# Last feed-forward stage: high and low latent halves as one 512-column moving operand

## What is computed

```python
def ffn_half(h, mod, k0, norm_w, wg, wu, wd):
    u = modulate(rmsnorm(h, norm_w), mod[:, k0, None], mod[:, k0 + 1, None])
    y = (jax.nn.silu(u @ wg) * (u @ wu)) @ wd
    return h + 0.5 * mod[:, k0 + 2, None] * y
```

## Time and profile before

| | us |
|---|---|
| median of 3 runs (lowest, highest) | 1979.12 (1977.79, 1980.22) |
| the profiled execution, its own time | 1976.28 |
| its span | 1974.6 |
| TensorE busy | 1942.9 (98%) |
| TensorE weight loads busy | 1649.4 (84%) |
| VectorE busy | 1262.6 (64%) |
| ScalarE busy | 795.4 (40%) |
| chain that ended last: TensorE's share | 92% |

### The profile page before, as it was taken

The page is one execution under the profiler, slowest core; times in us unless marked ns, Lnnn a source line. Parts: engine busy times, 40 slices in busy tenths (PEclk is TensorE's granted clock), DMA queues, the critical chain, the costliest instruction groups (busy, mean ns, idle before and its releaser), DMA issues.

```text
span 1974.6 us, 29022 instructions
## 1 busy us (share of the span) xinstructions
PE 1942.9 (98%) x10024; PEld 1649.4 (84%) x10024; DVE 1262.6 (64%) x2048; ACT 795.4 (40%) x1083; POOL 72.7 (4%) x142
## 2 busy tenths in 40 slices
PE   7999999999999999999999999999999998999998
PEld 2888888888888888888888888888888897999998
DVE  3667576676665466667566675755757678575555
ACT  2422222345554323532222353223224576456444
POOL 0000000000000000000000000000100000000000
PEclk9999999999999999999999999999999999999999
DMA  7345445433223243345454534444544333545554
GB/s 311 107 150 190 139 162 177 158 105 111 71 69 112 87 139 121 111 139 202 138 160 168 161 96 151 169 160 141 205 140 129 99 105 105 178 149 182 183 184 154
DMA packets 78664, 287.39 MB, mean 146 GB/s; under 512 B 8768, under 2 KB 10048, under 8 KB 77824
## 3 DMA queue, kind: packets, MB, share of 16 engines
q1 hardware_dynamic: 58912, 212.89, 32.5%
q0 software_dynamic: 19392, 73.34, 11.4%
q10 hardware_dynamic: 288, 0.18, 0.0%
HBM read 285.34 MB, written 1.05 MB: 145 GB/s over the span
## 4 chain that ended last, share of the span: by engine, by line
PE 92%; DVE 3%; DMA 2%; issue 1%; ACT 1%; ACTq 0%; DVEq 0%; SPq 0%
PE bank L333 26%; PE bank L334 26%; PE bank L335 26%; DMA raw<-weights 2%; PE bank L689 1%; PE bank L496 1%; PE bank L556 1%; PE bank L550 1%; PE bank L551 1%; ACT w_hi L712 1%; DVE S L1186 1%; PE bank L633 1%; PE bank L361 1%; PE bank L417 1%; PE bank L411 0%
## 5 line engine op out<-in xcount | busy, mean ns | idle before, releaser
L333 PE MATMUL bank<-u_hi,w_hi 128*128 128x512 f32 (+1 forms) x1824 | 664.0, 364 | 0.4 <-DVE w_lo L980 0.4
L334 PE MATMUL bank<-u_lo,w_hi 128*128 128x512 f32 (+1 forms) x1824 | 654.7, 359 | 0.0
L335 PE MATMUL bank<-u_hi,w_lo 128*128 128x512 f32 (+1 forms) x1824 | 654.6, 359 | 0.0
L980 DVE TENSOR_TENSOR w_lo<-raw,w_hi 128x1024 fp32r<-128x1024 f32 x384 | 469.1, 1223 | 245.8 <-ACT w_hi L712 216.5
L712 ACT ACTIVATE w_hi<-raw 128x1024 fp32r<-128x1024 f32 x384 | 405.1, 1056 | 435.1 <-DMA raw<-weights 434.4
L333 PEld LDWEIGHTS bank<-u_hi,w_hi 128*128 128x128 f32 x1824 | 344.5, 189 | 51.5 <-DVE w_lo L980 1.0
L335 PEld LDWEIGHTS bank<-u_hi,w_lo 128*128 128x128 f32 x1824 | 344.3, 189 | 51.3
L334 PEld LDWEIGHTS bank<-u_lo,w_hi 128*128 128x128 f32 x1824 | 344.6, 189 | 50.3 <-issue 0.7
L333 PE MATMUL bank<-hid_hi,w_hi 128*128 128x512 f32 (+1 forms) x832 | 299.1, 360 | 0.7 <-DVE w_lo L980 0.5
L991 DVE SCALAR_TENSOR_TENSOR junk<-ada_raw,silu_c 128x1024 bf16<-128x1024 f32 x256 | 298.2, 1220 | 0.5 <-DVE junk L991 0.5
L335 PE MATMUL bank<-hid_hi,w_lo 128*128 128x512 f32 (+1 forms) x832 | 298.2, 358 | 0.0
(11 more groups left out here) (162 smaller groups left out, 1504.5 us busy)
## 6 DMA issues: line engine op xcount, KB each, us to landing
raw<-weights SPq DMA_DIRECT2D x384, 512.0 KB, 3.5
ada_raw<-adaw POOLq DMA_DIRECT2D x128, 512.0 KB, 4.3
start_w<-weights SPq DMA_DIRECT2D x8, 1024.0 KB, 12.5
box<-box POOLq DMA_DIRECT2D x4, 1024.0 KB, 8.0
h<-resid SPq DMA_DIRECT2D x1, 2048.0 KB, 19.5
silu_c<-c POOLq DMA_DIRECT2D x1, 1024.0 KB, 5.2
out<-sig_a SPq DMA_DIRECT2D x8, 128.0 KB, 2.0
poolw<-poolw POOLq DMA_DIRECT2D x2, 256.0 KB, 10.0
```

The source lines that it names most:

```text
L333: pe.matmul(ps, w_hi[:, slot, k, :], hi(k), start=first, stop=False)
L334: pe.matmul(ps, w_hi[:, slot, k, :], lo(k), start=False, stop=False)
L335: mm = pe.matmul(ps, w_lo[:, slot, k, :], hi(k), start=False, stop=last)
L980: dve.tensor_tensor(view(w_lo, (j % RING) * UNIT, [1, UNIT]), raw[:, j % RING, :], view(w_hi, (j % RING) * UNIT, [1, UNIT]).bitcast(F32), ...
```

## The change

`u_hi` and `u_lo` become two halves of one tensor, `u_both` (at the same addresses as before). In the last feed-forward block, gate and up units take two matmuls per k in place of three: the high weights against the high and the low activations as one moving operand of 2 x 256 columns, written to both halves of the 512-column bank, and the low weights against the high activations (256 columns), added to the first half of the bank. The first four k of `abreast` stay as they were. The two halves of a bank are added on the way out: ACT copies the second halves of the up bank and the gate bank into the unused second halves of `hid_t` and `silu_t`, DVE adds the first halves of the banks to them, then Silu and the product read these sums from SBUF. Two semaphores are new: `s_low` (ACT to DVE) and `s_sum` (DVE to ACT and to DVE itself). Down units and all blocks over 512 tokens are as before.

```diff
-        u_hi, u_hi_at = sb("u_hi", [P, ND, ALL], F32R)
-        u_lo, _ = sb("u_lo", [P, ND, ALL], F32R)
+        u_both, u_hi_at = sb("u_both", [P, 2, ND, ALL], F32R)
+        u_hi, u_lo = u_both[:, 0], u_both[:, 1]
...
+            def half_latent(ps, slot, k, start, stop):
+
+                pe.matmul(ps[:], w_hi[:, slot, k, :], view(u_both, k * ALL, [ND * ALL, 2], [1, TOK]), start=start,
+                          stop=False, skip_group_check=True)
+                return pe.matmul(ps[:, 0:TOK], w_lo[:, slot, k, :], u_hi[:, k, 0:TOK], start=False, stop=stop,
+                                 skip_group_check=True)
+
+            def unit_latent(ps, slot, unit_wait):
+
+                pe.wait_ge(s_lo, unit_wait - START)
+                for k in range(ND):
+                    mm = half_latent(ps, slot, k, k == 0, k == ND - 1)
+                mm.then_inc(s_used, 1)
...
                 for g in range(AHEAD):
                     for k in range(side_by_side, ND):
                         pe.wait_ge(s_ulo, at + k + 1)
+                        if nt == TOK:
+                            mm = half_latent(bank[g], g, k, False, k == ND - 1)
+                            continue
...
                     for j in (2 * b, 2 * b + 1):
+                        if ntok == TOK:
+                            unit_latent(bank[j], j, i * 4 + (base + j + 1))
+                            continue
                         half(bank[j][:, 0:ntok], j, 0, ND, hi, lo, i * 4 + (base + j + 1), done=True)
...
-                        half(bank[3][:, 0:ntok], 3, 0, ND, hi, lo, base + 4, done=True)
+                        if ntok == TOK:
+                            unit_latent(bank[3], 3, base + 4)
+                        else:
+                            half(bank[3][:, 0:ntok], 3, 0, ND, hi, lo, base + 4, done=True)
...
                             act.wait_ge(s_used, i * 4 + (base + 2 * b + 2))
-                            act.activation(silu_t[:, b, 0:nt], bank[2 * b][:, 0:nt], ACT.Silu).then_inc(s_silu, 1)
+                            if last_ffn:
+                                for n_bank, low in ((2 * b + 1, hid_t), (2 * b, silu_t)):
+                                    ins = act.activation(low[:, b, TOK:ALL], bank[n_bank][:, TOK:ALL], ACT.Copy)
+                                ins.then_inc(s_low, 1)
+                                act.wait_ge(s_sum, i * 2 + (hid - hid_count(layer, which) + b + 1))
+                                act.activation(silu_t[:, b, 0:nt], silu_t[:, b, TOK:ALL], ACT.Silu).then_inc(s_silu, 1)
+                            else:
+                                act.activation(silu_t[:, b, 0:nt], bank[2 * b][:, 0:nt], ACT.Silu).then_inc(s_silu, 1)
...
                             split_lo(base, i, 2 * b + AHEAD)
+                            if last_ffn:
+                                at_sum = i * 2 + (hid - hid_count(layer, which) + b + 1)
+                                dve.wait_ge(s_low, at_sum)
+                                for n_bank, low in ((2 * b + 1, hid_t), (2 * b, silu_t)):
+                                    ins = dve.tensor_tensor(low[:, b, TOK:ALL], low[:, b, TOK:ALL],
+                                                            bank[n_bank][:, 0:TOK], ALU.add)
+                                ins.then_inc(s_sum, 1)
+                                dve.wait_ge(s_sum, at_sum)
                             dve.wait_ge(s_silu, i * 2 + (hid + b + 1))
 
-                            dve.tensor_tensor(hid_t[:, b, 0:nt], silu_t[:, b, 0:nt], bank[2 * b + 1][:, 0:nt],
+                            up = hid_t[:, b, TOK:ALL] if last_ffn else bank[2 * b + 1][:, 0:nt]
+                            dve.tensor_tensor(hid_t[:, b, 0:nt], silu_t[:, b, 0:nt], up,
                                               ALU.mult).then_inc(s_up_free, 1)
```

More of the change, by code:

```diff
@@ L204, in program @@
         s_silu = sem("silu_ready")
+        s_low = sem("low_halves_out")
+        s_sum = sem("halves_added")
         s_hid_hi = sem("hid_hi_ready")
```

## The result

Over six runs each on the same chips the changed kernel took 1983.63 us (median, 1981.22 to 1987.11) against 1978.09 us (1975.88 to 1980.22): ratio 1.0032, 95% interval 1.0020 to 1.0043, so slower by 4.0 to 8.5 us, the lower end lying just on the 0.2% that the prediction took as the limit of what can be told. The forecast was 1984.2 us, with 0.60 on slower. The profiled execution took 1981.22 us in place of 1976.28.

What follows compares the result with a forecast made beforehand. TensorE, busy 98% of the span, was taken as the bound. Part one +3.63, ends of the parts +4.49 and matmuls -2.99 sum to +5.1 us; put on the median 1979.12 that gave 1984.2 us, range 1980.0 to 1989.5.

Steps and rivals of the forecast that it cites:

- Ends of the parts: First down unit of each part waits for the last `hid_lo`: 1.43, 1.43 and 1.63 us more, +4.49 together.
- The chain: From TensorE leaving a gate/up pair to `hid_lo`: copies, additions, Silu, product and splits, all 1.63 us later than before.
- Part one, the mechanism: First part's gate/up: ACT and DVE in turn, with two table loads per round, become the bound instead of TensorE.
- The round: ACT-DVE loop in part one with both table loads: 12.31 us, where TensorE needs 11.09.
- Part one, the size: First down unit of part one starts at 1822.62 in place of 1818.99: +3.63 us, saved matmuls already lost.
- the anchor: Start of part one's sum: sixth unit's weights land by 1784.36 as before, and later rounds are counted from there.
- The matmuls: Gate/up k-step falls from 360.0 to 346.7 ns; over 28 units in parts two and three, -2.99 us.
- the second run: Rival: wide operand's second 256-column run costs a matmul's fixed part; k-step 360 ns, total 1987.2 us, chance 0.12.
- Nothing spare in parts two and three: ACT-DVE loop there needs 5.53 us where TensorE gives 5.55, so it just holds and TensorE's gain stays.
- The rival without loads: Copies let the loader keep one table, so part one gives 0.0; sum +1.5, 1980.6 us, chance 0.16.
- The rival with the hand-off covered: Between a pair's end and `hid_lo`, growth under 0.35 us causes no stalls; 1974.6 us, chance 0.08.

Runs made afterwards that it cites:

- The hand-off alone: Changed kernel with three matmuls per k as before, keeping the copies (scaled by zero) and additions; one execution 1984.07 us, block 200.94 us.
- the sums left out: Changed kernel without copies, additions and their semaphores, so the high-weights, low-activations product is missing from gate and up; one execution 1978.18 us, block 191.45 us.
- in fours: Changed kernel with four wide matmuls, then four narrow ones, twice per gate or up unit; one execution 1980.51 us, block 198.13 us.
- x4: Changed kernel with one tiny Silu ahead of part one, one table load in place of eight; one execution 1979.86 us, block 196.03 us.
- x5: Kernel before the change with one tiny Silu ahead of the last block's part one; one execution 1978.35 us, block 193.13 us.
- x11: Kernel before the change with one table load ahead of part one, timed over 12 runs: 1978.04 us, ratio 1.0002 (0.9991 to 1.0013).

## Why the prediction was right, and where not

- **Direction and total: right.** +5.1 us forecast, +4.9 in the profiled execution, +5.5 between the medians; that is outside the 4.0 us of no change, as forecast. The interval's lower end lies on that line and not beyond it.
- **Ends of the parts: right.** 1.43, 1.43 and 1.63 forecast, 1.41, 1.34 and 1.44 measured. The third is the whole stretch: the wait itself grew by 1.51 us (the matmul that needs the last `hid_lo` starts 3.75 us into the stretch in place of 2.24), and the waits behind it are together a little shorter. That a wait of this length can bring the clock down was not in the prediction. The chain was read from one pair and two rows of the mixer; it came out 0.08 us shorter than forecast. The hand-off alone and the sums left out show that these waits are its doing.
- **Part one, the mechanism: right.** The round was put at 12.31 us and is 12.16; ACT's second load does not wait for the sum, it starts at 1803.98 right behind the copies. Leaving the loads out of the new kernel takes 2.6 us off, out of the old one 0.6.
- **Part one, the size: 3.63 forecast, 2.17 measured.** The step that failed is the anchor: "whose weights land by 1784.36 and will again". ACT started that split at 1783.50, released by its weights, 0.9 us earlier, and every later round stands on it. Of these 0.9 us, 0.6 is that the split comes 7.23 us after the last `u_lo` in place of 7.85, and 0.3 that the block's first matmul came late, with the low clock ahead of it. Most of the rest of the 1.5 us is the rounds, 0.15 each. Over all runs the split's start moves by 0.8 us, so that this term can't be read more finely from one trace.
- **The matmuls: mis-sized by half.** "I take 226.7 + 120.0 = 346.7": in parts two and three a k-step is 353.4 ns, so they give 1.49 us, not 2.99. The sum of the two rows was not wrong as a pace, for it is met at the end of part one; it was wrong to take it for the only one. The one cause that the prediction named for a dearer step, the second run, is excluded by two runs. By the Trainium skill, page "TensorE: Matmul & The Clock Gate", section "Back-to-back issue gap", whose formula is for an isolated matmul gap, a dropped instruction would be worth 2.5 ns. The runs give 6.6 or 13.3 ns for a k-step by turns and 9.2 in fours, so the measurements decide against that figure too.
- **Two errors against each other.** Part one came out 1.5 us better than forecast and the matmuls 1.5 us worse. That the total fits to 0.2 us is luck. A total that fits is no proof of its terms; only the table by stretches shows it.
- **Nothing spare in parts two and three: right.** No wait for a gate or up unit's `w_lo` occurred there. With a pair of 5.65 us in place of 5.55 the loop of ACT and DVE had 0.1 us more room than forecast, so the dearer k-step may have shielded it; in fours, at 5.61, it held too, and at 5.55 no run with this hand-off in parts two and three tested it.
- **The rival without loads** did not happen: the trace of after still has four loads of 1.28 us at each of two lines. Its value was tested in the run with one load. The block is +2.2 against before, where the rival gave +1.5: the dearer k-steps of parts two and three add 1.5, part one and the ends take off 0.4 each.
- **The rival with the hand-off covered** says in one breath that the chain may grow by 0.35 us and that 0.20 are free. The second is right, since its own sum takes off the 0.15 for a released matmul. Nothing hangs on it: the chain grew by 1.55.

Open: what decides between the two paces of wide and narrow matmuls by turns, and why wide ones in a row here start 232 ns apart and not 226.7. Grouping removes 2.6 of the 6.7 ns in parts two and three. One difference stays untested: in `half` two matmuls in a row have the same tile of high weights, here no two have.

## What to carry to other kernels

Work moved from a busy engine to two half-idle ones is paid by the length of the chain through them, not by their shares: write the steps of one round with starts relative to the moment the producer leaves, and compare the end of each with when it is due. Look at the last round of a loop apart from the others, where no further round covers the chain, and give TensorE there something that does not need the last result. A wait there can cost more than its length: behind 1.8 us of it the clock fell in three executions of six. When engines wait on each other, let the hand-off go in halves, the half that starts the longer rest first.

## What was not expected of the hardware

- A matmul of 512 columns and one of 256 by turns have two steady paces in the same program. They take 353.4 ns in parts two and three, and 346.7, what the two widths alone (226.7 and 120.0) add up to, at the end of part one; four and four by turns take 350.8.
- Behind a wait in which TensorE had been idle for 1.80 us, three of six executions had a stretch at a granted clock of 0.50 (fifteen or sixteen matmuls of 256 columns 213 ns apart in place of 120); the fall came 0.9 to 1.5 us after the wait's end.
- A moving operand in two runs of 256, with 16 KB per partition between their starts, streams as fast as one run of 512 (45.23 against 45.23 us for 256 matmuls).
- Eight loads of ACT's tables, 1.28 us each, arise because a loop is entered with another table than it leaves; one tiny Silu ahead of the loop leaves one in place of eight (`x4`, `x5`, `x11`).
